# A first token tile in chunk order: split weights, two column groups at once, and a reordered load queue

## The reference, cut to what matters

```python
def mix_inputs(x, norm_g, w_in):
    z = rmsnorm(x, norm_g) @ w_in            # w_in: 1024 x 1792, fp32
    q = z[..., :512]; k = z[..., 512:640]; v = z[..., 640:768]
    u = gelu(z[..., 768:1280]); vg = gelu(z[..., 1280:])
```

## Time and profile before

| | us |
|---|---|
| median of 3 runs | 715.99 (715.69 to 718.16) |
| the profiled execution's own time | 715.4 |
| its span | 713.7 |
| TensorE busy | 692.3 (97% of the span) |
| VectorE busy | 555.3 (78%) |
| ScalarE busy | 451.4 (63%) |
| GpSimd busy | 152.3 (21%) |

### The profile page before, as it was taken

One profiled execution on the slowest core, in us unless ns is written; L12 is line 12 of the kernel. 1 busy time (PEld: TensorE's weight loads), 2 busy tenths in 40 slices (PEclk: granted clock), 3 DMA queues, 4 the chain that ended last, 5 costly groups with the idle time before them and its releaser, 6 DMA issues.

```text
span 713.7 us, 11899 instructions
## 1 busy us (share of the span) xinstructions
PE 692.3 (97%) x3816; PEld 540.9 (76%) x3816; DVE 555.3 (78%) x890; ACT 451.4 (63%) x714; POOL 152.3 (21%) x157
## 2 busy tenths in 40 slices
PE   7999999999999999999988999999999999999995
PEld 4777777887778778777777888888888888888842
DVE  4775866866858875363887999999999999999857
ACT  7645354453465643122245888898889888898745
POOL 1010010110110131000014233333333333341114
PEclk9999999999999999999999999999999999999998
DMA  9993830330311626635339999999999999998758
GB/s 350 267 308 96 196 89 0 88 88 0 88 59 68 237 96 235 261 128 187 112 137 353 415 415 412 411 392 388 403 392 381 380 393 393 366 404 339 268 197 357
DMA packets 80922, 181.10 MB, mean 254 GB/s; under 512 B 41720, under 2 KB 45984, under 8 KB 72696
## 3 DMA queue, kind: packets, MB, share of 16 engines
q1 hardware_dynamic: 71384, 163.12, 63.0%
q0 software_dynamic: 9216, 16.93, 6.3%
q10 hardware_dynamic: 288, 0.62, 0.3%
HBM read 162.89 MB, written 34.39 MB: 276 GB/s over the span
## 4 chain that ended last, share of the span: by engine, by line
PE 85%; DVE 4%; DMA 4%; ACT 2%; issue 2%; SPq 1%; POOL 1%; DVEq 0%; ACTq 0%; POOLq 0%
PE psZ L1391 24%; PE psZ L901 20%; PE psS L1418 12%; PE psZ L1092 10%; PE psT L831 6%; PE psOG L831 2%; PE psOG L974 2%; PE psS L942 2%; DMA wo_in<-w_out 1%; PE psOG L1223 1%; PE psOG L983 1%; DMA yy<-y_d 1%; PE psOG L873 1%; DVE x1a L2692 1%; PE psT L1181 1%
## 5 line engine op out<-in xcount | busy, mean ns | idle before, releaser
L2388 DVE TENSOR_TENSOR wg_lo<-wg,wg_hi 128x1024 fp32r<-128x1024 f32 x128 | 150.7, 1218 | 2.0 <-ACT wg_hi L1531 2.0
L1531 ACT ACTIVATE wg_hi<-wg 128x1024 fp32r<-128x1024 f32 x128 | 128.8, 1062 | 3.6 <-DVE small L2550 1.6
L1391 PE MATMUL psZ<-wg_hi,xg_hi 128*128 128x512 f32 x252 | 101.4, 402 | 0.0
L1391 PE MATMUL psZ<-wg_hi,xg_lo 128*128 128x512 f32 x252 | 99.0, 393 | 0.0
L1391 PE MATMUL psZ<-wg_lo,xg_hi 128*128 128x512 f32 x252 | 99.0, 393 | 0.0
L901 PE MATMUL psZ<-wi_hi,xT_hi 128*128 128x512 f32 (+1 forms) x240 | 90.0, 375 | 1.0 <-DVE wi_lo L1963 1.0
L2774 POOL DMA_INDIRECT y_d<-y_t,idx_dst x32 | 48.9, 1528 | 188.5 <-ACT y_t L1531 188.5
L2577 DVE TENSOR_TENSOR wd_lo<-wd,wd_hi 128x2048 fp32r<-128x2048 f32 x31 | 71.1, 2292 | 21.0 <-ACT wd_hi L1531 21.0
L901 PE MATMUL psZ<-wi_lo,xT_hi 128*128 128x512 f32 (+1 forms) x240 | 87.2, 364 | 0.0
L901 PE MATMUL psZ<-wi_hi,xT_lo 128*128 128x512 f32 (+1 forms) x240 | 87.2, 363 | 0.0
L2770 POOL DMA_INDIRECT xg<-h_d,idx_src x32 | 58.5, 1830 | 22.2 <-issue 13.7
(11 more groups left out here) (354 smaller groups left out, 1346.3 us busy)
## 6 DMA issues: line engine op xcount, KB each, us to landing
wg<-w_gate SPq DMA_DIRECT2D x32, 1024.0 KB, 9.9
wg<-w_up SPq DMA_DIRECT2D x32, 1024.0 KB, 17.4
wd<-w_down SPq DMA_DIRECT2D x32, 1024.0 KB, 13.1
y_d<-wo_stage SPq DMA_DIRECT2D x1, 4608.0 KB
wi_raw<-w_in SPq DMA_DIRECT2D x4, 1024.0 KB, 14.1
x_t<-x_rows SPq DMA_DIRECT2D x8, 512.0 KB, 4.0
mix_d<-mix_t SPq DMA_DIRECT2D x8, 512.0 KB, 3.0
m_t<-mix_d SPq DMA_DIRECT2D x8, 512.0 KB, 3.7
```

Of the source, the lines that this page charges most:

```text
L1391: last = nc.tensor.matmul(psZ[z][:], a[:, c, :], w, start=(n == 0), stop=(n == 3 * DC - 1))
L1531: return nc.scalar.activation(out, in_, ACT.Copy)
L2388: tt(wg_lo[k][:, :, c, :], wg[k][:, :, c, :], wg_hi[p][:].bitcast(F32), ALU.subtract).then_inc(s_wgl, 1)
```

## The change

The changes all lie in the first tile and in the queue around it.

- `w_in`'s first and last pieces are loaded as two halves, one chunk each; x of tile 0 as two halves of 512 columns, of which TensorE awaits the first ahead of the sample transposes.
- ScalarE and VectorE split, and signal, chunk by chunk (16 steps in place of 8); the second half of x is split behind the first two weight chunks; the square of x stands further back on ScalarE.
- TensorE takes the products of tile 0 chunk by chunk with both column groups of the half (`z_first(m)`): per chunk four products with `wi_hi`, then two with `wi_lo`, so both groups end together. The sample rows' products go by single chunks, the lower columns as 4 x 192 in place of 3 x 256. Three products of the identity with itself (`warm`) stand between the transposes.
- SyncE loads `xb` of tile 1 right behind the weights and `cst`, without its waits; the zeros to `y_d` go behind `z_d` instead of ahead of it; `z_d` is stored in 8 pieces.
- ScalarE's `z_out` moves from behind `values(0)` to behind `x_hi(1, 1)`.
- `xsT` moves to the memory of `mix_t`, and some semaphores are shared.

```diff
@@ SyncE @@
             for n in range(1, N_WI):
                 load_wi(n)
             sp.dma_start(cst[:, C_CS + HD:], consts[:, C_CS + HD:C_END]).then_inc(s_small, 16)
-            sp.dma_start(ws_raw[:], w_s.rearrange("g t s -> t g s")).then_inc(s_ws, 16)
...
-            sp.wait_ge(s_xTp, 2)
-            sp.wait_ge(s_zs, N_WI + 1)
             load_xb(1)
+            sp.dma_start(ws_raw[:], w_s.rearrange("g t s -> t g s")).then_inc(s_ws, 16)
...
             stage1(0)
-            sp.wait_ge(s_zx, 1)
+            sp.wait_ge(s_zs, 2 * N_WI + 2)
+            for m, (c0, c1) in enumerate(WI_COLS):
+                w = (c1 - c0) // 4
+                for j in range(4):
+                    sp.dma_start(z_d[:, c0 + w * j:c0 + w * (j + 1)], zq_t[32 * j:32 * j + N_SAMPLE, ZQ[m]:ZQ[m] + w])\
+                        .then_inc(s_zy, 16)
+            sp.wait_ge(s_pset, 1)
             sp.dma_start(y_d.rearrange("(t p k) n -> p t k n", p=P, k=2)[:, :, 0], wo_stage[0][:, 0:D].unsqueeze(1).to_broadcast([P, T, D]))\
-                .then_inc(s_zy, 16)
-            sp.wait_ge(s_zs, N_WI + 2)
...
@@ TensorE @@
+            def z_first(m):
+                outs = (psZ[0], psZ[1][:, 0:256]) if m == 0 else (psS[:, 0:512], psS[:, 512:1024])
+                cols = [slice(c0 - WI_COLS[m][0], c0 - WI_COLS[m][0] + n) for c0, n in Z_GROUPS[2 * m:2 * m + 2]]
+                for c in range(DC):
+                    k = DC * m + c
+                    if k % 2 == 1 and k + 2 < 2 * N_WI:
+                        z_sample(k + 1)
+                        z_sample(k + 2)
+                    if m == 0 and c % (DC // 2) == 0:
+                        pe.wait_ge(s_xh, 1 + c // (DC // 2))
+                        pe.wait_ge(s_xl, 1 + c // (DC // 2))
+                    pe.wait_ge(s_whi, k + 1)
+                    for i in range(2):
+                        nc.tensor.matmul(outs[i][:], xT_hi[:, c, :], wi_hi[m][:, c, cols[i]], start=(c == 0), stop=False)
+                        nc.tensor.matmul(outs[i][:], xT_lo[:, c, :], wi_hi[m][:, c, cols[i]], start=False, stop=False)
+                    pe.wait_ge(s_wlo, k + 1)
+                    for i in range(2):
+                        last = nc.tensor.matmul(outs[i][:], xT_hi[:, c, :], wi_lo[m][:, c, cols[i]], start=False,
+                                                stop=(c == DC - 1))
...
@@ ScalarE @@
-            def split(n):
+            def split(k):
 
-                act.wait_ge(s_wi[n], 16)
-                for c in range(2):
-                    g = 2 * (n % 4) + c
-                    last = nc.scalar.activation(wi_piece(wi_hi, n)[:, c, :], raw_piece(n)[:, c, :],
-                                                ACT.Copy, scale=gmix[:, g:g + 1])
-                last.then_inc(s_whi, 1)
+                n, c, g = k // 2, k % 2, k % DC
+                act.wait_ge(s_wi_end[n // 4] if k in (1, 2 * N_WI - 1) else s_wi[n], 16)
+                nc.scalar.activation(wi_piece(wi_hi, n)[:, c, :], raw_piece(n)[:, c, :], ACT.Copy, scale=gmix[:, g:g + 1])\
+                    .then_inc(s_whi, 1)
...
@@ VectorE @@
+                n, c, g = k // 2, k % 2, k % DC
+                dve.wait_ge(s_wi_end[n // 4] if k in (1, 2 * N_WI - 1) else s_wi[n], 16)
+                dve.wait_ge(s_whi, k + 1)
+                if k >= 2:
+                    dve.wait_ge(s_zs, k + 2)
```

More of the change, by code:

```diff
@@ new lines, in z_sample @@
+            def z_sample(k):
+                if k == 0:
+                    pe.wait_ge(s_xsT, 1)
+                n, c, m = k // 2, k % DC, k // DC
+                pe.wait_ge(s_wi_end[m] if k in (1, 2 * N_WI - 1) else s_wi[n], 16)
+                c0, c1 = WI_COLS[m]
+                w = (c1 - c0) // 4
+                for j in range(4):
+                    last = nc.tensor.matmul(psO[32 * j:32 * j + N_SAMPLE, ZQ[m]:ZQ[m] + w], xsT[:, c, :],
+                                            raw_piece(n)[:, k % 2, w * j:w * (j + 1)], start=(c == 0), stop=(c == DC - 1),
+                                            skip_group_check=True)
+                last.then_inc(s_zs, 1)
@@ new lines, in z_first @@
+            def z_first(m):
[17 more added lines that the diff above has]
+                                                stop=(c == DC - 1))
+                        if c == DC - 1:
+                            last.then_inc(s_z, 1)
+                    if m == 1 and c == DC // 2 - 1:
+                        last.then_inc(s_zm, 1)
@@ L878, in z_group @@
             def z_group(t, g):
                 c0, n = Z_GROUPS[g]
-                first = isinstance(t, int) and t == 0
-                out = psS[:, 512 * (g - 2):512 * (g - 2) + n] if first and g >= 2 else psZ[g % 2][:, 0:n]
-                if not first:
-                    if g == 2:
-                        pe.wait_ge(s_qr, t + 1)
-                    elif g == 3:
-                        pe.wait_ge(s_kr, t + 1)
-                    else:
-                        pe.wait_ge(s_u if g == 0 else s_vg, t)
+                out = psZ[g % 2][:, 0:n]
@@ L889, in z_group @@
+                if g == 2:
+                    pe.wait_ge(s_qr, t + 1)
+                elif g == 3:
+                    pe.wait_ge(s_kr, t + 1)
+                else:
+                    pe.wait_ge(s_u if g == 0 else s_vg, t)
                 k = 0
@@ L1024, in _ @@
             z_sample(1)
-            stage1(0)
+            z_first(0)
+            z_first(1)
+            t_qk(0)
+            set_up()
+            scores(0, 0)
             stage1(1)
@@ L1656, in stage1 @@
                         set_up_cache()
-                else:
-                    for n in range(4, N_WI):
-                        split(n)
                 values(t)
@@ L1668, in stage1 @@
                     p_out(t - 1, 1)
-                else:
-                    z_out()
                 if end:
@@ L1683, in stage1 @@
                     o_out(t - 1)
+                else:
+                    z_out()
                 shift(t)
@@ L1687, in _ @@
             x_hi(0, 0)
-            x_hi(0, 1)
             split(0)
             split(1)
+            x_hi(0, 1)
+            for k in range(2, 6):
+                split(k)
+            for k in range(6, 11):
+                split(k)
             square(0)
-            split(2)
-            split(3)
+            for k in range(11, 2 * N_WI):
+                split(k)
             stage1(0)
@@ L2129, in stage1 @@
                     norm_p(t - 1, 0)
-                else:
-                    dve.wait_ge(s_id, 16)
-                    for n in range(4, N_WI):
-                        split(n)
                 rope_q(t)
@@ L2161, in _ @@
             x_lo(0, 0)
-            x_lo(0, 1)
             split(0)
             split(1)
-            split(2)
-            split(3)
+            x_lo(0, 1)
+            for k in range(2, 6):
+                split(k)
+            for k in range(6, 2 * N_WI):
+                split(k)
             stage1(0)
```

136 lines of the change are left out of this document (54 added, 82 removed).

## The result

| | before | changed |
|---|---|---|
| median | 718.16 (715.69 to 719.28, 7 runs) | 722.85 (720.80 to 725.19, 7 runs) |
| profiled execution, own time | 715.4 | 723.82 |
| its span | 713.7 | 721.7 |
| mean granted clock in it | 0.997 | 0.997 |

The ratio is 1.0072, with a 95% interval of 1.0046 to 1.0098: 5.2 us slower. The forecast was 2.5 us slower, a time of 718.5 and a range up to 720.4. The sign of the shift and its place were right, its size was half of what came. The time itself lies 4.35 above the forecast's 718.5; 2.2 of that is the base, since the kernel before has a median of 718.16 over seven runs and had 715.99 over three, so I go by the ratio.

The account below looks back on a forecast made before the run. The prediction took TensorE to bound the kernel, so a shift of tile 2's start reaches the end: 715.4 + 2.5 = 717.9, with 0.6 up to the median a forecast of 718.5 us, range 714.6 to 720.4.

Parts of the forecast that it names:

- the start of the products: Tile 0: TensorE's products of x with the weights start at 9.0 us, 2.3 earlier than before.
- the worst case: Upper bound for the start of tile 0's products: 9.9 us, as late as before but for one block.
- TensorE's work: Tile 0: products and sample rows take 26.75 us, so the products end at 35.75, 1.85 earlier.
- VectorE's tail: End of tile 0: split parts end at 33.6, rotation at 37.5, now the path; tile 1's products at 41.1, 0.4 later.
- The queue: SyncE behind z_out: y_d issued at 45.9, xb of tile 2 in at 66.3, tile 2's products at 70.7, 2.5 later.
- Sum: Whole kernel: tile 2's 2.5 us delay reaches the end, 717.9 for the profiled run, 718.5 as the forecast median.
- The range: Whole kernel: 714.6 to 720.4 us, from just below the first rival to the bulk of the second.
- the load comes in time: Rival, ahead of tile 2: xb is in time and a front gain of 1.1 us stays, 714.9; chance 0.20.
- the small tables arrive last: Rival, ahead of tile 1's turn of x: tables land after 37.5 and delay it; landing at 38.5 gives 719.5; chance 0.12.
- the clock falls in the new idle time: Rival, ahead of tile 2: TensorE idles some 2.4 us and its clock falls, costing 2.8, 721.3; chance 0.04.

Follow-up runs that it names:

- zero_warm: turn_ahead with early TensorE products of zeros: three ahead of the sample transposes, one behind them, one ahead of the first sample rows; ratio 0.9974 to the kernel before.
- front_undone: The changed kernel with x of tile 0 in one load, no warm-up products, and first and last weight pieces loaded whole; ratio 1.0069 to the kernel before.
- x_whole: The changed kernel with x of tile 0 in one load, nothing else undone; ratio 1.0067 to the kernel before.
- samples_ahead: y_d_early with the last four sample rows (chunks 12 to 15) one step sooner; ratio 1.0046 to the kernel before.
- after_again: The changed kernel unaltered, run and profiled a second time (the second profile); ratio 1.0080 to the kernel before, span 718.5 us.
- no_warm: The changed kernel without its three warm-up products; ratio 1.0064 to the kernel before.
- y_d_early: The changed kernel with the zeros to y_d back ahead of the wait for z_out and the z_d stores; ratio 1.0061 to the kernel before.
- late_y_d: zero_warm with the zeros to y_d put back behind the z_d stores, as in the changed kernel; ratio 1.0032 to the kernel before.
- queue_own: The kernel before with z_out behind tile 1's second x_hi, y_d behind z_d, and y_d off the semaphore shared with the z_d stores; ratio 1.0050.
- turn_ahead: rope_between with tile 1's first turn of x ahead of split part 15, its x_lo behind that part, x_hi ahead of the first GELU; ratio 0.9985 to before.
- rope_between: front_undone with y_d early, the small tables' wait moved back, and the rotation of q and k between VectorE's last split parts; ratio 0.9989 to the kernel before.

## Why the prediction was right and wrong

The step that failed is the first, the start of the products: forecast at 9.0 and at 9.9 in the worst case, measured at 10.07 and 11.05. With it came a pace that held in one execution and not in the other. The path behind it was as forecast. Of the 2.24 that tile 2 came later than forecast in the second profile, 1.65 is made by the time tile 0's products end (1.07 by their start, 0.6 in the products), and the rest is the load's way behind `y_d`. Taken by its own steps, with the second profile of the changed kernel unless said.

- **Start of the products, 9.0.** The step that failed: 10.07 (11.05 in the first profile). The step took the first half of x at 3.9 and it landed at 4.72 (4.40); with x in one load the wait is for `xs_t` and ends at 3.4. And it priced a warm-up product at a quarter of a microsecond from eight transposes in 1.97, when the profile lists such an fp32 product as two: 1.45 for three. These two terms are 0.8 and 0.7 too small; the sample rows took 1.1 and gave back 0.3. In the first profile there is also the wait for the second half of x, 0.76, a term that the sum does not have.
- **TensorE's work, 26.75.** Nearly right where the pace is full: 37.4 - 10.07 = 27.3, in zero_warm 36.3 - 9.05 = 27.3. In the first profile it was 28.7, since the slow stretch that the earlier trace rows show on the transposes (1.97 for eight) lay on the products. The forecast moved the products forward towards that stretch and priced them at the late pace, 0.235 each from the earlier trace rows at 13.81 and later, with nothing to show that products at 9 us would have it. That this went well in the second profile is luck.
- **VectorE's tail.** Right in kind: the last split part ended 2.05 ahead of the last product, forecast 2.15; the rotation was on the path, the turn of x at 39.12, 1.6 later than the 37.5 forecast, all of it inherited. Tile 1's products came 4.4 behind the turn instead of 3.6, as the clock was at 0.50 from 40.5 to 43.5; in the first profile, where it stayed at 1.00, they came 3.64 behind it. So tile 1 is at 43.55 and 45.12 against a forecast of 41.1. The small tables were taken to land at 36.3; where a wait shows it, they landed at 38.16 (front_undone), 39.78 (x_whole) and 40.40 (samples_ahead, with `y_d` already flowing). In the changed kernel VectorE came as late as they did or later, so this cost nothing.
- **The queue.** Right in kind and nearly in size. `z_out`'s four copies took 2.16, the eight `z_d` stores 2.65 (2.85), and from the issue of `y_d` to the turn it was 21.35, forecast 20.4 (other runs: 20.8 to 22.3). From the turn to tile 2's products 4.06, forecast 4.4.
- **Sum.** Tile 2 at 72.94 in place of 70.7: 1.6 from a `y_d` that was issued late with the front (47.53 against 45.9), 0.95 from the load's way behind it, less 0.35. In the first profile it is 74.92: 3.8 from `y_d` (49.67), 0.8, less 0.35. The second makes 4.8 against the profile of before, and the times say 5.2 with an interval from 3.3 to 7.0: nothing is left over that could be measured.
- **The range** held the front at its worst at 9.9, because I took "as late as before" for an upper bound. It isn't one: what comes before it had been changed in three places.

The rivals. That the load comes in time fell: VectorE waited 5.2 for it. That the small tables arrive last was false for the change itself, since VectorE came later than they, and true as soon as it was quicker (samples_ahead, x_whole, front_undone). That the clock falls in the new idle time I gave 0.04, on the strength of one gap of 1.49 in the earlier trace rows without a fall, and I looked for it ahead of tile 2 alone. It fell ahead of tile 1 in four of the five profiles of the changed kernel and its undone versions (after_again, x_whole, no_warm, front_undone; not in the first profile) and in samples_ahead, not in y_d_early. The prediction does not have that place. The Trainium skill's rule (TensorE: Matmul & The Clock Gate, section The HAM clock gate), that an idle engine goes back to 1.2 GHz and must warm up again, holds in these traces: in late_y_d the granted clock went to 0.50 within a gap of 2.7 us. Its executions differ by 2.6 us between higher and lower mean clock; the price I had put on it was 2.8. It is no certainty either: in the first profile of the changed kernel TensorE waited 2.53 ahead of tile 2 and the clock stayed at 1.00.

What stays open: why the second half of x came at 8.61 in one execution and not in the other, what sets the moment between 8.7 and 14.5 us at which products reach full pace, and why the clock falls behind some gaps and not behind others of the same length.

## What to carry to other kernels

A small load queued behind a large store on the same queue lands only after the store (here 21 us after the store's issue, the store itself 13.9); count from the large transfer's issue to the small one's landing (here 20.8 to 22.3 us in seven profiles) and compare it with the slack. Two delays that end in the same wait don't add in full, so taking one away shows little until the other is gone too; to price one, test it in a kernel where nothing else is late. A term taken from a row holds for the state in which that row ran: work that is moved to the start of the program, or behind a new gap, may run at half pace.

## What the runs showed of the hardware

- The same products took 0.235 us at full pace and 0.43 at half pace at the start, while the granted clock's row read 1.00 over both; the durations tell the pace there, the row does not. In later gaps the row did fall, to 0.50: ahead of tile 1 in five profiles, ahead of tile 2 in late_y_d and queue_own.
- The start's slow stretch ended between 8.7 and 14.5 us: by 8.67 in front_undone (gaps of 0.53 and 0.34 in TensorE's work), at 12.2 in no_warm (no gap, later start), at 12.9 in turn_ahead (gaps of 0.50 and 0.61), at 14.2 in rope_between (a gap of 1.26), by 10.07 and at 14.5 in two executions of one kernel. The Trainium skill, in the section named above, says that throttled is the default and activity releases it, and that the moment varies from run to run; both profiles of the changed kernel agree, with 4.4 us between them, far more than the half microsecond that the section gives for it. With products of zeros from 1.80 us on, full pace stood at 9.05 in zero_warm and, after one slow product, at 9.57 in late_y_d. That they bring it forward is not shown: front_undone had it at 8.67 without them.
- Issuing is not free while a large transfer on the queue drains: with `y_d` (4.7 MB) ahead of it, SyncE stood 9.79 us on `w_re`, and 16.4 us on the four `xb` loads, half a megabyte together, behind the weights.
